# Sample caches and keys of a hybrid decoder step turned on VectorE in 32x32 blocks

## What is computed

```python
def compress_blocks(kv, pe, w1, b1, w2):
    seg = kv[:, :n_seg * CMP_STRIDE].reshape(B, n_seg, CMP_STRIDE, 2, NSA_KV_HEADS, NSA_HEAD_DIM)
    proj = jnp.einsum('bnscgd,cmsdh->mbncgh', seg, w1r)
    h = sum(proj[m][:, m:m + nc] for m in range(r)) + (pe_bias + b1)[None, None, :, None, :]
    out = jnp.einsum('bncgh,chd->bncgd', jax.nn.gelu(h), w2)

def nsa_core(qg, tq, kc, vc, tc_end, kb, vb, kw, vw, tw, gates):
    p_c = masked_softmax(jnp.einsum('bqgrd,bngd->bqgrn', qg, kc), ...)
    imp = jnp.einsum('bqgn,nj->bqgj', p_c.sum(axis=3), overlap_matrix(nc, nb))
    _, idx = lax.top_k(score, min(SLC_TOP_N, nb))        # score = imp, forced blocks raised
    o = g[..., 0:1] * o_c + g[..., 1:2] * o_s + g[..., 2:3] * o_w
```

## Time and profile before

| what | us |
|---|---|
| median of 3 runs (lowest, highest) | 1277.18 (1277.05, 1279.13) |
| the profiled execution, its span | 1275.8 |
| TensorE busy in it | 1210.0 |
| VectorE, ScalarE, GpSimd busy | 717.7, 434.3, 118.3 |

### The profile page before, as it was taken

How to read it: one execution, slowest core, us unless ns; L and a number is a source line. 1 busy time by engine, 2 the same in 40 slices (tenths; PEclk the granted TensorE clock), 3 DMA queues, 4 the chain that set the end, 5 groups by cost and what they waited for, 6 DMA issues and landing times.

```text
span 1275.8 us, 20912 instructions
## 1 busy us (share of the span) xinstructions
PE 1210.0 (95%) x7670; PEld 952.7 (75%) x7670; DVE 717.7 (56%) x1752; ACT 434.3 (34%) x1063; POOL 118.3 (9%) x178
## 2 busy tenths in 40 slices
PE   7899999679989999999999999899999999999996
PEld 4677776556767777777877878678887888878884
DVE  4733334887765675666666553654546454472335
ACT  2111103436656665675666521322111111100004
POOL 4200000534430000000000000200002000000000
PEclk9899999789998999999999999999999999999998
DMA  9633430431008166246423511612222121212201
GB/s 366 238 132 132 161 143 33 153 120 84 1 3 358 68 267 261 105 193 280 159 120 148 214 68 43 221 67 74 92 69 95 66 99 55 108 52 91 91 1 70
DMA packets 22872, 162.69 MB, mean 128 GB/s; under 512 B 2792, under 2 KB 9032, under 8 KB 12632
## 3 DMA queue, kind: packets, MB, share of 16 engines
q1 hardware_dynamic: 19928, 92.42, 19.8%
q0 software_dynamic: 2736, 69.36, 13.0%
q10 hardware_dynamic: 144, 0.04, 0.0%
...
## 4 chain that ended last, share of the span: by engine, by line
PE 84%; DVE 8%; ACT 4%; issue 2%; DMA 1%; POOL 0%; ACTq 0%; DVEq 0%; POOLq 0%
PE PS L344 76%; PE PS L1013 4%; PE PS L1172 3%; PE PS L1092 1%; ACT trunk L1709 1%; ACT zreg L1569 1%; DMA ringreg<-in_w_ada_dram 1%; DVE w L2315 1%; DVE sreg L2363 1%; DVE zreg L2133 1%; DVE sreg L1963 0%; DVE creg L1963 0%; ACT zreg L1559 0%; ACT ringreg L1538 0%; ACT sreg L1409 0%
## 5 line engine op out<-in xcount | busy, mean ns | idle before, releaser
L344 PE MATMUL PS<-mixreg,w 128*128 128x272 f32 (+1 forms) x596 | 139.2, 385 | 10.0 <-DVE mixreg L1958 4.2
L344 PE MATMUL PS<-creg,ringreg 128*128 128x272 f32 (+1 forms) x564 | 144.2, 400 | 3.4 <-ACT creg L1417 2.7
L344 PE MATMUL PS<-zreg,w 128*128 128x256 f32 (+2 forms) x544 | 140.9, 390 | 4.7 <-DVE zreg L2161 2.9
L344 PEld LDWEIGHTS PS<-mixreg,w 128*128 128x128 f32 x596 | 110.1, 195 | 31.9 <-issue 8.3
L344 PE MATMUL PS<-mixreg,ringreg 128*128 128x272 f32 (+1 forms) x532 | 130.2, 398 | 1.0 <-DVE sreg L2333 1.0
L344 PEld LDWEIGHTS PS<-creg,ringreg 128*128 128x128 f32 (+1 forms) x564 | 104.4, 187 | 33.2 <-issue 9.8
L344 PEld LDWEIGHTS PS<-mixreg,ringreg 128*128 128x128 f32 (+1 forms) x532 | 99.1, 189 | 23.0 <-DVE sreg L2333 1.5
L344 PE MATMUL PS<-zreg 128*128 128x256 f32 (+4 forms) x320 | 105.2, 411 | 6.1 <-DVE ringreg L2035 2.9
L344 PEld LDWEIGHTS PS<-zreg,w 128*128 128x128 f32 (+1 forms) x544 | 90.9, 189 | 22.2 <-issue 5.2
L1569 ACT ACTIVATE zreg<-PS 128x512 f32<-128x512 f32 x128 | 75.7, 592 | 69.2 <-PE PS L1013 69.2
L344 PE MATMUL PS<-mixreg,sreg 128*128 128x272 f32 x352 | 87.2, 395 | 0.0
(11 more groups left out here) (381 smaller groups left out, 1835.0 us busy)
## 6 DMA issues: line engine op xcount, KB each, us to landing
ringreg<-in_w_ada_dram SPq DMA_DIRECT2D x24, 1024.0 KB, 7.3
ringreg<-in_w_f_dram SPq DMA_DIRECT2D x22, 1024.0 KB, 4.9
ringreg<-in_w_in_dram SPq DMA_DIRECT2D x11, 1024.0 KB, 5.0
...
ringreg<-in_w_o_dram SPq DMA_DIRECT2D x4, 1024.0 KB, 8.9
...
```

The lines of the kernel that those rows point to most:

```text
L344: return nc.tensor.matmul(o, lhsT, rhs, start=start, stop=stop, **kw)
```

## The change

A block transpose on VectorE (`nc.vector.transpose`) swaps rows and columns inside each 32x32 block, from SBUF to SBUF.

- **Finer gather.** `cmp_load` issues eight gathers of 128 rows of 4 KB for each batch instead of one of 128 rows of 32 KB, by a second index table. The cache then lies so that block transposes alone bring channels onto partitions. `W1` is reloaded for that layout by 32 DMAs of SyncE after the prompt's compression; a copy of the queries in four blocks comes by 16 more (`zR`).
- **Turning.** VectorE's `turn_in(b, k)`, 8 for each batch, turns 1024 elements a partition and adds pairs (512). `segments`, `pair`, `seg_copy` and `differences` are gone. TensorE multiplies in `outer` (4 matmuls of 256 columns) and `inner` (2), 8 steps. What the differences did is now done on the results (`hidden_in` has three operations, `hidden_odd` two).
- **Keys.** VectorE's `keys_in` turns the selection keys (four of 1024 elements) and the window's (512) into the freed compression buffer; `block_scores` is 64 matmuls of 32 channels by 32 query rows by 288 columns.
- **Buffers.** Compression and selection caches share three buffers in turn. `cmp_load(b+1)` waits for `pv_done` of b-1, in the middle of batch b; `slc_load(b+1)` for the scores of b.
- **Moved between engines.** For the second half (values) GELU's products go to GpSimd, with two more ScalarE operations each; the copies of the turned probabilities, value rows and outputs go from VectorE to ScalarE. The loops are written out. The tail is split in `tail_turned` and `tail_values`. The scaled queries are made before the prompt's attention. Two output tiles more stand between the parts of the last tail, and `w_o` may load earlier.

The diff's core:

```diff
@@ GpSimd
             def cmp_load(b):
-                if b >= 2:
-                    pool.wait_ge(sem("seg_pair"), 16 * (b - 1))
-                nc.gpsimd.indirect_dma_start(out=(RC if b % 2 == 0 else RR)[:, :], out_offset=None, in_=a["cmp"],
+                for n in range(8):
+                    nc.gpsimd.indirect_dma_start(out=cmp_buf(b)[:, n * XB:(n + 1) * XB], out_offset=None, in_=cmp_table,
+                                                 in_offset=bass.IndirectOffsetOnAxis(ap=idxc[:, n // 4, n % 4, b:b + 1], axis=0)
+                                                 ).then_inc(sem(f"cmp_in{b % 2}"), 16)
...
+            for b in range(DB + 1):
+                if b and b < DB:
+                    pool.wait_ge(sem("cmp_sq"), 2 * b)
+                    nc.gpsimd.tensor_tensor(hgx, hgx, HXS[:, :, :], ALU.mult).then_inc(sem("cmp_poly"), 1)
+                    pool.wait_ge(sem("cmp_tanh"), 2 * b)
+                    nc.gpsimd.tensor_tensor(hgx, hgx, HXS[:, :, :], ALU.mult).then_inc(sem("cmp_g"), 1)
+                if b + 1 < DB:
+                    if b:
+                        pool.wait_ge(sem("pv_done"), b)
+                    cmp_load(b + 1)
+                    pool.wait_ge(sem("sc_s"), b + 1)
+                    slc_load(b + 1)
@@ TensorE
+            def outer(b, k):
+                n, c, q = NX * b + k, k // 4, k % 4
+                x = row_parts(n)
+                even, odd = firsts(c)
+                if q == 0 and b:
+                    pe.wait_ge(sem("cmp_hx"), 6 * (b - 1) + 3 * c + 3)
+                pe.wait_ge(sem("seg_t"), n + 1)
+                for h in range(2):
+                    matmul(even, W1[:, c, 1, 2 * q + h, :], x[:, :, h, 0, :], q == 0 and h == 0, q == 3 and h == 1, skip_group_check=True)
+                    matmul(odd, W1[:, c, 0, 2 * q + h, :], x[:, :, h, 1, :], False, q == 3 and h == 1, skip_group_check=True)
+            def inner(b, k):
...
+                if q == 0 and (b or c):
+                    pe.wait_ge(sem("cmp_hx"), 6 * b + 3 * c)
+                pe.wait_ge(sem("seg_sum"), n + 1)
...
+            def block_scores(b):
...
+                for k in range(4):
+                    for i in range(4):
+                        for a_ in range(QG):
+                            matmul(PS[group(a_), sc_banks[i], 0:KW], qb[group(i), k, :], kt[group(i), k, a_, :], k == 0, k == 3)
...
+                for c in range(2):
+                    outer(b, 4 * c)
+                    if c and b:
+                        tail_turned(b - 1)
+                    outer(b, 4 * c + 1)
+                    inner(b, 4 * c)
+                    inner(b, 4 * c + 1)
+                    if c:
+                        if b:
+                            tail_values(b - 1)
+                        cmp_keys(b)
...
@@ VectorE
+            def turn_in(b, k):
+                n, c, q = NX * b + k, k // 4, k % 4
+                if k == 0:
+                    dve.wait_ge(sem(f"cmp_in{b % 2}"), 128 * (b // 2 + 1))
+                if n >= XR:
+                    dve.wait_ge(sem("cmp_mm"), n - XR + 1)
+                nc.vector.transpose(turned_rows(n).rearrange("p (x s r) -> p s x r", x=4, s=8),
+                                    cmp_rows(b)[:, :, q, c, :].rearrange("p s (x d) -> p s x d", x=4)).then_inc(sem("seg_t"), 1)
+                dve.wait_ge(sem("seg_t"), n + 1)
+                x = turned_rows(n).rearrange("p (x e n) -> p x e n", x=4, e=2)
+                nc.vector.tensor_tensor(row_sums(n).rearrange("p (x n) -> p x n", x=4), x[:, :, 0, :], x[:, :, 1, :], ALU.add).then_inc(sem("seg_sum"), 1)
...
+            for b in range(DB):
+                if b:
+                    hidden_in(b - 1, 1)
+                    chosen(b - 1)
+                turn_in(b, 4)
+                if b:
+                    masked(b - 1)
+                turn_in(b, 5)
+                if b:
+                    maxima(b - 1)
+                turn_in(b, 6)
+                hidden_in(b, 0)
+                turn_in(b, 7)
+                gelu_poly(b)
+                keys_in(b, 0)
...
+                cmp_softmax(b)
+                if b + 1 < DB:
+                    for k in range(XR):
+                        turn_in(b + 1, k)
```

704 lines of the change are left out of this document (337 added, 367 removed).

## The result

The changed kernel takes 1308.56 us (median of 4 runs, 1305.61 to 1312.19) against 1277.47 for the kernel before (1277.05 to 1279.13): a ratio of 1.0241, 95% interval 1.0220 to 1.0262. The forecast was 1273.6, from 1254 to 1296, so the time lies outside the range and the likelier sign was the wrong one. The profiled execution has a span of 1308.2 against 1275.8.

A forecast was written before the change was run, and what follows sets the result against it. TensorE bounds the kernel now; afterwards a ring through the buffers would, at 46.5 us a batch. Attention +5.0, first release -2.3, six periods +7.6 and the end -13.9 make -3.6: 1277.2 to 1273.6 us, range 1254 to 1296.

The forecast's parts named there:

- a ring: Sample batches: buffer release, gather, VectorE, ScalarE and TensorE steps until the next release set the period, 46.5 us against 45.22.
- D: Rival, sample batches: TensorE stays the limit, period 36 if the gather came early enough, 1211 us; chance 0.04.
- E: Rival, gathers: eight small ones pay their fixed part one after the other, 13.5 us longer a batch, 1355 us; chance 0.02.
- the turn: VectorE's block transpose of 1024 elements: taken at 1.18 us, like a one-to-one operation of equal size.
- C: Rival, VectorE: the block transpose takes two passes, 2.3 us, adding 6.7 and more a batch, 1311 us; chance 0.08.
- A: Rival, VectorE: the block transpose takes 0.64 us instead of 1.18, period 43.3, 1254.4 us; chance 0.13.
- behind the ring: From the seventh buffer release to the end of the last tail and output tiles: 33.9 us instead of 47.8, -13.9.
- the attention behind eight gathers: Prompt's attention: its scaled identities queue behind eight gathers on GpSimd, 4.1 to 7.0 us too late; taken at +5.0.
- step 6: TensorE's turned probabilities and values with one outer and two inner steps between: 8.65 us, low clock allowed for separately at 1.1.
- Rival B: Sample batches: low clock falls on TensorE's probabilities and values, and small rows are slow; period 49, 1288.6 us; chance 0.25.
- step 1: Sample batches, the gather from buffer release to landing: 13.7 to 15.3 us, taken at 14.5.
- the first round: Stage start to first buffer release: 60 us instead of 62.3, -2.3.

The follow-up runs named there:

- e5: Changed kernel with only the order of work altered on TensorE, VectorE and ScalarE, to shorten the ring: 1259.27 us, ratio 0.9859 to the kernel before.
- e10: Changed kernel with each of the first four turns of a batch done twice: 1324.66 us, ratio 1.0382 to the kernel before.
- e11: Changed kernel with VectorE's masks and maxima of the previous batch ahead of the fifth and sixth turns: 1276.97 us, ratio 0.9991 to the kernel before.
- e4_busy: Changed kernel with zero-weight matmuls added in TensorE's waits, from the second batch on: 1300.07 us, ratio 1.0181 to the kernel before.
- e3: Changed kernel with one 4 MB gather in place of eight of 0.5 MB, compressed output not the reference's: 1297.41 us, ratio 1.0140 to the kernel before.
- e2: Changed kernel with VectorE's hidden rows, choice, masks and maxima ahead of the next batch's four turns: 1295.27 us, ratio 1.0116 to the kernel before.
- e12: Changed kernel with a new order on three engines, two repairs ahead of the batches, and weight sums on VectorE instead of GpSimd: 1243.06 us, ratio 0.9727.

## Why the prediction was wrong, by its own steps

**Right: what bounds the stage after the change.** TensorE gives up the bound and a ring through gather, turns, choice, masks, exponentials, probabilities and values takes over. Every releaser named for it stands in the trace, and e5, e10 and e11 move the start of the turned probabilities by what the list of steps says. The rival that TensorE stays the limit (D) is out; so is E, since the eight small gathers overlap. TensorE's own work was forecast at 33.3; in e4_busy, at clock 1.00, it is 45.41 less 28 added matmuls of 0.43, 33.4. The scores in 32x32 tiles, taken at 2.7, took 3.20 (3.1 with less waiting) and stand in no step of the ring, as said.

**Right: the turn.** The largest unknown term, 1.18, is 1.24; two passes (C) and half a pass (A) fall. The estimate from the Trainium skill, "Vector Engine (DVE) Microarchitecture Reference", § 3.8, 1.07, was the farther one.

**Right: behind the ring.** -12.9 against -13.9 (by its own rows the 47.8 of the kernel before is 47.6). And the attention behind eight gathers: +6.3 against +5.0, within the 4.1 to 7.0 given.

**Wrong: step 6, by the low clock (+3.3 a period, less the 1.1 allowed).** The prediction saw the wait in front of the turned probabilities, saw in the earlier trace rows that such a piece is followed by a clock of 0.50, bounded the cost by 0 and 4.3, and then took 1.1. The argument for the low value was that the clock may have fallen earlier and come back by then. It did fall earlier, at 575 to 581, and had come back to 1.00 at 583, but the wait of 3.3 made it fall a second time, right on the ring. With e4, 12.5 instead of 9.15 is its price in the round shown, 3.3; in the mean of the rounds it is 12.1 against 9.3, 2.8. Six times that is 17 to 20 us, of which the forecast had 6.6. Rival B was this mechanism, with a period of 49 and 1288.6, and had 0.25. Its upper end was added up wrongly: 46.5 + 3.2 and a gather of 15.3, 0.8 more, give 50.5 and not 49.5, which is 1297.6, and the measured period of 50.2 lies below it. (C's sum is off too: six times 6.7 are 40 and not 37. Neither changes the forecast.) B should have been the forecast: the row that spoke for it was a measured one, and what spoke against it was only a possibility.

**Wrong: step 1, the gather (+1.5; +1.6 in the mean of six rounds).** It was priced by the landing of the selected cache's gather, 13.4, where the other cache's gather into one of its buffers had a median of 14.9 on the same page. One by one, the two gathers of the kernel before that were in flight alone (issued at 281.19 and 407.10) landed in 13.3 and 13.2, those of its middle batches in 13.3 to 15.0. The grain, for which the sum had added 0.8, costs 0.2 to 0.7 by e3; the other 1.7 are in the base. 15.2 to 17.0 is what the rounds of all runs with eight gathers show (e2 aside, where the turn waits for something else), and the upper end of the range, 15.3, was too low as well. Why even one gather takes 15.4 here is open.

**Missed: the start (+7.3).** Sixteen loads of 1 KB were joined to a semaphore for which ScalarE and VectorE wait before their first work. The part on the change looked at added instructions in the stage and on SyncE's queue, and passed over the count in a wait that grew from 144 to 400. Nothing in the prediction's range covers it.

**Missed: the first round (+1.9 against -2.3).** 3.8 of the 4.2 are the length of the pair sum that stood behind GpSimd's additions (e12); the low clock on the first step 6 (0.50 from 450 to 455) would account for the rest and more, and how these overlap was not resolved.

Put together: B's 1288.6, with 50.2 instead of 49 for the period (+7.2), 7.3 for the start, 4.2 for the first round, 1.3 for the attention and 1.0 behind the ring, is 1309.6, and 1308.6 was measured. The terms are differences read from the two traces, so that they add up checks the reading and not the causes; those rest on the experiments. Of the 36 us between forecast and trace 22 lie in the six periods, 7.3 in the start, 4.2 in the first round, and the rest in the other two.

**Two expectations of the experiments failed in the same manner.** e10 and e11 were worked out by adding a cost to the ring and holding the clock still; the clock moved against it each time, by about 3 us.
